# Attention of a hybrid decoder step: two heads of a pair side by side in the matmul array, V stationary, probabilities scaled before their transposes

## The reference, cut to what matters

```python
ATTN_PATTERNS = ((128, 1), (512, 4), (2048, 16))      # window, dilation; 8 heads of 64 each
def dilated_mixer(u, past, w_qkv, w_o):
    qkv = (u @ w_qkv).reshape(b, l, 3, 3, 8, 64)       # group, q/k/v, head, 64
    for g, (win, dil) in enumerate(ATTN_PATTERNS):
        s = q @ k.T + alibi bias, keys by stride dil within win
        lse = logsumexp(s); p = exp(s - lse); o_g = p @ v
    w = softmax over the groups of their lse
    return sum_g(w_g * o_g) @ w_o
```

## Time and profile before

| | us |
|---|---|
| median of 3 runs | 2786.29 (2784.93 to 2808.14) |
| profiled execution, own time | 2783.1 |
| its span | 2781.0 |
| TensorE busy in the span | 2640.1 (95%) |
| VectorE, ScalarE, GpSimd busy | 1672.3, 1275.4, 877.5 |
| the four attention turns, with the last projection | 1938.1 to 2360.5 |

### The profile page before, as it was taken

The page is one execution under the profiler, slowest core; times in us unless marked ns, Lnnn a source line. Parts: engine busy times, 40 slices in busy tenths (PEclk is TensorE's granted clock), DMA queues, the critical chain, the costliest instruction groups (busy, mean ns, idle before and its releaser), DMA issues.

```text
span 2781.0 us, 48966 instructions
## 1 busy us (share of the span) xinstructions
PE 2640.1 (95%) x19399; PEld 2551.3 (92%) x19399; DVE 1672.3 (60%) x2599; ACT 1275.4 (46%) x2139; POOL 877.5 (32%) x677
## 2 busy tenths in 40 slices
PE   6999998999999977999998999999999998899997
PEld 6999998899999967999998999998989886899997
DVE  6744757777777767843756835753343445772674
ACT  6634732444444436743736734632222224662561
POOL 4232233444444423232234232233222220423222
PEclk9999999999999988999999999999999999999999
DMA  6644622222222214644625635625222221562652
GB/s 165 160 118 126 154 82 95 79 87 70 80 91 84 92 65 130 166 114 122 169 90 132 161 110 129 157 77 181 99 96 103 87 90 42 136 160 95 152 137 73
DMA packets 92108, 316.77 MB, mean 114 GB/s; under 512 B 12240, under 2 KB 13904, under 8 KB 77456
## 3 DMA queue, kind: packets, MB, share of 16 engines
q1 hardware_dynamic: 52752, 242.78, 25.3%
q0 software_dynamic: 39168, 71.32, 15.2%
HBM read 223.44 MB, written 19.32 MB: 87 GB/s over the span
## 4 chain that ended last, share of the span: by engine, by line
PE 81%; DVE 7%; issue 4%; ACT 3%; POOL 2%; DMA 1%; SPq 0%; DVEq 0%; POOLq 0%; ACTq 0%
PE ps L1289 11%; PE ps L1281 11%; PE ps L1283 11%; PE ps L1306 7%; PE ps L1307 7%; PE ps L1313 7%; PE ps L1209 5%; PE ps L1215 5%; PE ps L1210 5%; PE ps L1618 1%; PE ps L1561 1%; PE ps L1475 1%; POOL sb_wl L600 1%; PE ps L1476 1%; PE ps L1477 1%
## 5 line engine op out<-in xcount | busy, mean ns | idle before, releaser
L1283 PE MATMUL ps<-sb_ual,sb_hw 128*128 128x288 f32 x2240 | 619.8, 297 | 0.0
L1281 PE MATMUL ps<-sb_uah,sb_hw 128*128 128x288 f32 x2240 | 618.1, 299 | 1.2 <-ACT sb_hw L789 0.8
L600 POOL TENSOR_TENSOR sb_wl<-sb_raw,sb_wh 128x1024 fp32r<-128x1024 f32 (+1 forms) x106 | 267.6, 2529 | 571.5 <-ACT sb_wh L758 571.5
L644 POOL DMA_DIRECT2D sb_lw<-sb_rawf x240 | 207.1, 864 | 703.8 <-ACT sb_lw L790 683.8
L1281 PEld LDWEIGHTS ps<-sb_uah,sb_hw 128*128 128x128 f32 x2240 | 425.4, 190 | 2.4 <-ACT sb_hw L789 2.0
L1283 PEld LDWEIGHTS ps<-sb_ual,sb_hw 128*128 128x128 f32 x2240 | 424.2, 189 | 0.0
L1289 PE MATMUL ps<-sb_uah,sb_lw 128*128 128x288 f32 x2240 | 391.0, 297 | 12.8 <-DMA sb_lw<-sb_rawf 12.8
L1209 PE MATMUL ps<-sb_uh,sb_wh 128*128 128x256 f32 (+1 forms) x1360 | 377.3, 305 | 8.9 <-ACT sb_wh L758 6.4
L1306 PE MATMUL ps<-sb_hh,sb_hw 128*128 128x288 f32 x1408 | 381.0, 298 | 4.4 <-DVE sb_x L1926 4.4
L1307 PE MATMUL ps<-sb_hl,sb_hw 128*128 128x288 f32 x1408 | 381.1, 297 | 0.0
L1210 PE MATMUL ps<-sb_ul,sb_wh 128*128 128x256 f32 (+1 forms) x1360 | 372.7, 300 | 0.0
(11 more groups left out here) (269 smaller groups left out, 5024.1 us busy)
## 6 DMA issues: line engine op xcount, KB each, us to landing
sb_rawf<-w_ffn_in SPq DMA_DIRECT2D x88, 1024.0 KB, 4.9
sb_lw<-sb_rawf POOLq DMA_DIRECT2D x272, 256.0 KB, 3.6
sb_raw<-w_ssd SPq DMA_DIRECT2D x64, 512.0 KB, 3.5
sb_rawf<-w_ffn_out SPq DMA_DIRECT2D x32, 768.0 KB, 4.2
sb_rawf<-w_ffn_out SPq DMA_DIRECT2D x32, 640.0 KB, 3.8
sb_raw<-w_att SPq DMA_DIRECT2D x40, 512.0 KB, 3.9
sb_h<-state SPq DMA_DIRECT2D x8, 1024.0 KB, 4.9
ssm_sample<-sb_h SPq DMA_DIRECT2D x8, 1024.0 KB, 4.8
```

Source lines behind the costliest of these rows:

```text
L600: pool.tensor_tensor(wl[parity][:, 0:width], raw[:, parity, 0:width], wh[parity][:, 0:width].bitcast(F32), ALU.subtract).then_inc(wl_done, 1)
L644: pool.dma_start(slot(lw, p), rawf[:, s % 2, i * BL:(i + 1) * BL], accum_op=ALU.add).then_inc(ld_in[i], 16)
L1281: pe.matmul(out, w[:, k * P:(k + 1) * P], uah[:, SIDE[p], k, :], start=begins and k == 0, stop=False, skip_group_check=True)
L1283: pe.matmul(out, w[:, k * P:(k + 1) * P], ual[:, SIDE[p], k, :], start=False, stop=False, skip_group_check=True)
```

## The change

- `scores` becomes `wide_scores(t)` and `narrow_scores(t)`: for a block t of queries both heads follow each other, head 0 in rows 0 to 63 of the array, head 1 in rows 64 to 127, each into a bank of its own.
- `normalize(e)` scales the probabilities `pr` (768 wide) by the reciprocal sum before they are transposed; `head_out`, `un` and the four transposes of `un` are gone.
- The twelve transposes of a block t go in three groups of four (`transposes(t, i)`), and ScalarE copies each group with one 512-wide copy (`probs_out(t, i)`). But for the last block and the last turn all groups use bank 2.
- `values(t)`: V is stationary (64 columns for each head, head 1 in columns 64 to 127), 128 columns of transposed probabilities move. The output has features on partitions, so `heads_out(t)` and `heads_low(t)` make its high and low part for the projection, strided into token order.
- Both sample stages go through the sequences in the order `BY_STRIP`, so that neighbours are in different strips. The sample group's own scores go into bank 2 with a step `sample_own` of their own.
- The output projection takes halves of 288 columns in token order, and VectorE adds each block to `x` with one operation.
- Order: in the first three turns `ahead(2t)` comes first in block t, then transposes and the next scores between them, then `ahead(2t+1)` and `values(t)`.

```diff
+BY_STRIP = (0, 2, 4, 6, 1, 3, 5, 7)
...
-                        nc.scalar.copy(pt[:, e % 2, 0:512], ps[:, 6, :])
-                        nc.scalar.copy(pt[:, e % 2, 512:768], ps[:, 7, 0:256]).then_inc(pt_done, 1)
+                        src = ps[:, turned_bank(t, i, last), :]
+                        if i == 1:
+                            nc.scalar.copy(pt[:, :, 512:768], two(src)).then_inc(pt_done, 1)
+                        else:
+                            nc.scalar.copy(pt[:, i // 2, 0:512], src).then_inc(pt_done, 1)
+
+                    def heads_out(t):
+                        act.wait_ge(pv_mm, c * 4 + (t + 1))
+                        nc.scalar.copy(perm(oh[:, 0:SEQ])[:, t, :], ps[:, head_bank(last), 0:P]).then_inc(oh_done, 1)
...
+                    def wide_scores(t):
+                        if t:
+                            pe.wait_ge(max_done, c * 8 + 2 * t)
+                        for j in range(2):
+                            r = slice(HD * j, HD * j + HD)
+                            pe.matmul(ps[:, 4 + j, :], qkv[r, 0, rows(t)], qkv[r, 1, 0:SEQ], start=True, stop=True)
...
+                        pe.wait_ge(pt_done, c * 12 + (3 * t + 3))
...
                         for k in range(6):
-                            v = vt[:, max(0, k - 3), k if k < 4 else t, r]
-                            ins = pe.matmul(ps[:, 2, 0:HD], pt[:, e % 2, rows(k)], v, start=k == 0, stop=k == 5)
+                            for j in range(2):
+                                r = slice(HD * j, HD * j + HD)
+                                v = vt[:, max(0, k - 3), k if k < 4 else t, r]
+                                ins = pe.matmul(ps[r, head_bank(last), 0:P], v, pt[:, j, rows(k)], start=k == 0, stop=k == 5)
...
-                            for b in range(NB):
-                                out = ps[32 * (b // 2):32 * (b // 2) + 32, 3, 0:P]
-                                for k in range(4):
+                            for k in range(4):
+                                for b in BY_STRIP:
+                                    out = ps[32 * (b // 2):32 * (b // 2) + 32, 3, 0:P]
...
+                        for t in range(CH):
+                            if t:
+                                pe.wait_ge(q_evac, c * 9 + (9 + 2 * t))
+                            ahead(2 * t)
+                            sample_step(2 * t)
+                            transposes(t, 0)
+                            if t < CH - 1:
+                                wide_scores(t + 1)
+                            transposes(t, 1)
+                            if t < CH - 1:
+                                narrow_scores(t + 1)
+                            transposes(t, 2)
+                            pe.wait_ge(q_evac, c * 9 + (10 + 2 * t))
+                            ahead(2 * t + 1)
+                            sample_step(2 * t + 1)
+                            values(t)
...
+                        V.tensor_scalar(pr[:, e % 2, :], pr[:, e % 2, :], rcp[:, e:e + 1], None, ALU.mult).then_inc(norm_done, 1)
...
+                        V.tensor_tensor(perm(ol[:, 0:SEQ])[:, t, :], ps[:, head_bank(last), 0:P],
+                                        perm(oh[:, 0:SEQ])[:, t, :].bitcast(F32), ALU.subtract).then_inc(ol_done, 1)
...
-                        xm = x[:, m, 0:SEQ].rearrange("p (a h t) -> p h t a", h=2, t=2)
-                        V.tensor_tensor(xm, xm, ps[:, b:b + 2, 0:QTR].rearrange("p h (t a) -> p h t a", t=2), ALU.add)
-                        V.tensor_tensor(x[:, m, SEQ:TOK], x[:, m, SEQ:TOK], ps[:, b + 1, QTR:QTR + SMP],
-                                        ALU.add).then_inc(ao_evac, 1)
+                        V.tensor_tensor(two(x[:, m, :]), two(x[:, m, :]), ps[:, b:b + 2, 0:HALF], ALU.add).then_inc(ao_evac, 1)
```

More of the change, by code:

```diff
@@ L250, in step_kernel @@
             stage = at("stage", [P, AHEAD, TOK])
-            un = at("un", [P, CH, P])
             oh = at("oh", [P, TOK], F32R)
@@ L1158, in sample_step @@
                             ins.then_inc(soh_done, 1)
[L1160 to L1175, removed]
+                    if last:
+                        for t in range(CH):
+                            for i in range(3):
+                                probs_out(t, i)
+                            sample_step((1, 2, 4, 6)[t])
+                            heads_out(t)
+                            if t < CH - 1:
+                                exps(2 * t + 2)
+                                exps(2 * t + 3)
+                                sample_step((6, 3, 5)[t])
+                    else:
+                        for t in range(CH):
+                            ahead(2 * t + 1)
+                            sample_step(2 * t)
+                            for i in range(3):
+                                probs_out(t, i)
+                            ahead(2 * t + 2)
+                            if t < CH - 1:
+                                exps(2 * t + 2)
+                                exps(2 * t + 3)
+                            sample_step(2 * t + 1)
+                            heads_out(t)
                         ahead(9)
@@ L1554, in ahead, with narrow_scores @@
                         product(c * 10 + u, u % 2, KD, uh, ul, (0, 1), SPLIT)
[L1556 to L1568, removed]
+                    def wide_scores(t):
[4 more added lines that the diff above has]
+                            pe.matmul(ps[:, 4 + j, :], qkv[r, 0, rows(t)], qkv[r, 1, 0:SEQ], start=True, stop=True)
+                    def narrow_scores(t):
+                        for g in (1, 2):
+                            for j in range(2):
+                                r = slice(HD * j, HD * j + HD)
+                                ins = pe.matmul(ps[:, 6 + j, rows(g - 1)], qkv[r, 3 * g, rows(t)],
+                                                qkv[r, 3 * g + 1, rows(t)], start=True, stop=True)
+                        ins.then_inc(sc_mm, 1)
                     pe.wait_ge(q_evac, c * 9 + 9)
@@ L1608, in values @@
[L1608 to L1616, removed]
-                            v = vt[:, max(0, k - 3), k if k < 4 else t, r]
-                            ins = pe.matmul(ps[:, 2, 0:HD], pt[:, e % 2, rows(k)], v, start=k == 0, stop=k == 5)
+                    wide_scores(0)
@@ new lines, in turn, with transposes @@
+                    narrow_scores(0)
+                    for g in range(AG):
+                        ins = pe.transpose(ps[0:SMP, 2, rows(g)], qkv[:, 3 * g + 2, SEQ:TOK], ident[:, :])
+                    ins.then_inc(vt_mm, 1)
+                    sample_scores()
+                    def transposes(t, i):
+                        n, bank = 3 * t + i, turned_bank(t, i, last)
+                        if i < 2:
+                            pe.wait_ge(norm_done, c * 8 + (2 * t + i + 1))
+                        if n == 0:
+                            pe.wait_ge(own_done, c + 1)
+                        elif t == CH - 1 and i:
+                            pe.wait_ge(max_done, c * 8 + 8)
+                        elif last:
+                            pe.wait_ge(pt_done, c * 12 + max(1, n - 1))
+                        elif i:
+                            pe.wait_ge(pt_done, c * 12 + n)
+                        else:
+                            pe.wait_ge(ol_done, c * 4 + t)
+                        for q, (j, k) in enumerate((((0, 0), (0, 1), (0, 2), (0, 3)), ((0, 4), (0, 5), (1, 4), (1, 5)),
+                                                    ((1, 0), (1, 1), (1, 2), (1, 3)))[i]):
+                            ins = pe.transpose(ps[:, bank, rows(q)], pr[:, j, rows(k)], ident[:, :])
+                        ins.then_inc(pt_mm, 1)
@@ new lines, in values @@
+                    def values(t):
+                        pe.wait_ge(pt_done, c * 12 + (3 * t + 3))
+                        if last and t:
+                            pe.wait_ge(ol_done, c * 4 + t)
+                        for k in range(6):
+                            for j in range(2):
+                                r = slice(HD * j, HD * j + HD)
+                                v = vt[:, max(0, k - 3), k if k < 4 else t, r]
+                                ins = pe.matmul(ps[r, head_bank(last), 0:P], v, pt[:, j, rows(k)], start=k == 0, stop=k == 5)
@@ L1648, in turn @@
                     if last:
[L1650 to L1656, removed]
-                    else:
[L1658 to L1674, removed]
+                        wide_scores(1)
+                        narrow_scores(1)
+                        for t in range(CH):
+                            for i in range(3):
+                                transposes(t, i)
+                            sample_step((0, 2, 4, 0)[t])
+                            values(t)
+                            if t < CH - 2:
+                                wide_scores(t + 2)
+                                narrow_scores(t + 2)
+                            sample_step((0, 3, 5, 0)[t])
+                    else:
```

(44 more changed lines are left out.)

145 lines of the change are left out of this document (70 added, 75 removed).

## The result

The changed kernel takes 2706.95 us (median of 4 runs, 2702.87 to 2707.93) against 2789.82 before (4 runs); the ratio is 0.9689, 95% interval 0.9642 to 0.9735. The profiled execution took 2702.87, its span is 2700.8. The forecast was 2713, 2698 to 2750.

What follows compares the result with a forecast made beforehand. TensorE was taken to bound the loop's three turns, the chain between engines the last. Three times -18.5 and -18 made -73.5: 2783.1 to 2709.6, plus 3.2 for the median of runs, 2713; range 2698 to 2750.

Steps and rivals of the forecast that it cites:

- the sum: All terms together: three turns of the loop -55.5, last turn with its projection -18, all -73.5 us.
- Values: Values of a block: the two heads' records run two at a time, 1.4 us, -5.4 a turn (bounds 0 and -5.4).
- Scores: Scores of a block: the heads' row groups overlap, 1.8 us in place of 3.0, -4.8 a turn (bounds 0 and -5.6).
- The rival without overlap: In the loop, score pairs don't run side by side: 2728; this or value pairs failing 22%, both 10%.
- Strip order: Both sample stages, neighbours in different strips: 2.3 us each from 5.28 and 5.92, -6.6 a turn (bounds -4.2 and -7.7).
- The projection: Output projection ending a loop turn: plain addition makes it TensorE-bound, 6.5 us in place of 9.2, -2.7 a turn.
- Added waits: New waits on TensorE's queue: +0.3 three times for bank 2, +0.9 at a turn's head; +1.8 a turn (+0.5 to +4).
- Scaling in the loop: VectorE's scaling of the probabilities in the loop's blocks: hidden, so costs nothing; uncovered it would be 1.8 a block.
- The last turn: Last turn up to its projection, bounded by VectorE's chain: 38.1 us in place of 53.5, -15.4 (bounds -10 and -17).
- the 5.0 at the end: Last turn, behind the last scaling: two groups of transposes, copies, values and the high and low parts, 5.0 us.
- The last projection: Projection after the last turn, VectorE-bound, 15.9 us: 0.58 less on each of eight blocks, partly overlapped, -2.6.
- The rival that ends slower: TensorE falls to half clock, 1.2 GHz, in the loop's turns after new waits; two turns give about 2813; 3%.

Runs made afterwards that it cites:

- control: The changed kernel itself, run again with nothing changed as a measure for the others: 2710.58 us, ratio 0.9734 against the kernel before.

## Why the prediction was right

The bound was read rightly: TensorE's own operations in the loop's turns, the chain between engines in the last. In the loop I had -18.5 a turn; measured -18.2, -19.6 and -20.9. Only turn 0 has a granted clock of 1.00 in both traces. The third turn of the kernel before, which the rows above leave out:

```profile
2171.10:2287.30 116.20, 114.54 (x822) 0.96 0.27 93
```

So the second and third turn went from 0.97 and 0.96 to 0.99 and 0.98, and the 1.4 and 2.7 us that they gave beyond turn 0 go with that. What the change itself gave in the loop is then about 54.6 of the 58.7 us (an estimate: three times turn 0), against 55.5 foretold.

The spans shrank by 80.2 us where the sum said 73.5. The 6.7 more are 3.2 in the loop, 1.1 in the last projection, 2.5 by which the attention stage began sooner and 0.9 behind it, less 0.9 in the last turn. None of them is a gain of the mechanism that the sum had missed; the first two go with the clock.

- Values: 1.4 a block foretold, 1.46 measured. What I took from the earlier trace rows, seven records in flight where one strip meets the next, held for halves of 64 columns, and the order by heads confirmed it.
- Scores: 1.8 a block foretold from 1.6 to 3.0. Wide 1.06, narrow 0.65 with its change of shape, and the transposes between them 0.15 longer each time: 1.9. The rival without overlap fell in the experiment with the wide scores apart.
- Strip order: 2.3 a stage foretold, 1.87 and 1.88 measured, near the bound of 1.75. The term was mis-sized by 0.9 a turn: it is -7.5, not -6.6.
- The projection: 6.5 foretold, 7.5 measured. I took the slower of the two engines and left out that with two pairs of banks they wait for each other. With three pairs it is 6.6. The term was -1.7 a turn, not -2.7. This miss and that of the strips nearly cancel, and that the loop's sum is so close is in part luck.
- Added waits, the term of +1.8: the wait at a turn's head was put at 0.9 and is 0.74. The one for bank 2 was put at 0.3; between the end of the copy, 1951.32 + 0.59, and the next transposes at 1951.96 it shows, but it costs 0.2 at most with the change of shape that is due anyway. Together that is about 1.3 (an estimate: 0.74 and three times 0.2).
- Scaling in the loop: covered, as foretold, with more room than I worked out.
- The last turn: 15.4 foretold, 14.5 (control: 16.1) measured, but not by the parts named. I put eight scalings, 7.2 us, on the chain. Without the scaling the turn is 0.5 shorter, and only two of the eight are on the control's chain (0.62 and 0.63). This step of the prediction was wrong. In place of the scalings stand TensorE's operations for which VectorE waits: 13.3 us of that chain's 41.1 are TensorE's (its rows added up), scores and transposes of 2.6 behind a block's maxima at full clock among them, and I had put TensorE only into the 5.0 at the end. The last turn's sum was right by luck: two errors met.
- The last projection: -2.6 foretold, -3.7 measured. From its first matmul to its last addition it is 15.7 in the kernel before, 14.6 with the permuted additions put back and 12.0 in the changed kernel: the additions are worth the 2.6. The other 1.1 goes with the clock. Its start in the kernel before, in the changed kernel (whole), and in the one with the wide scores apart:

```profile
2344.61:2347.80 3.19, 3.19 (x13) 0.51 0.03 5
```

```profile
2268.97:2280.99 12.02, 10.47 (x69) 1.00 0.08 13
```

```profile
2280.64:2285.90 5.26, 5.26 (x22) 0.50 0.01 3
```

  The last of these has the changed kernel's projection and took 13.3 for it, as did the one with three pairs, which also began with 5 us at half clock; the seven others with this projection began at full clock and took 12.0.
- The clock: in the loop's turns it was 1.00, 0.99 and 0.98 where it had been 1.00, 0.97 and 0.96. The rival that ends slower did not come about; the clock rather added to the gain, which no term of the sum had.

## What to carry to other kernels

Small matmuls that use half or a quarter of the array cost what they do because their neighbours use the same part. Look for the seam between two parts in the trace, count the records in flight there, and if they double, alternate the parts in program order, matmul by matmul; the seam is all that a block order gets. Where two engines pass a few blocks to and fro, the slower engine's time is the bound only with enough buffers. And of a chain with a wait, write down every operation that must stand in it: one that lies beside another adds nothing.

## What the runs showed of the hardware

Halves and quarters of the array took fp32 matmuls side by side with nearly no loss: two row groups 1.06 for 1.05, two column halves 1.46 for 24 records of 0.11, four strips 1.88 for 64. The page "TensorE: Matmul & The Clock Gate" of the Trainium skill (Part 3, The mechanism) has loads overlap only with matmuls of another row group. The values and the sample stages use the same rows throughout, and yet 24 records take 1.46 us and not 24 x 0.11, so the trace disagrees.

A copy on VectorE took six times as long beside an operation on GpSimd. In the kernel before, three copies of 576 columns from SBUF to SBUF took 3.40 us beside a subtraction on GpSimd; in the changed one they take 450 ns each; in turn 0 GpSimd is idle beside them. First the line's shortest, median and longest copy (ns) and the timeline of turn 0 before, then the line after:

```profile
L2325 DVE COPY sb_qkv<-sb_stage x9: 449/453/2671, 2036.0 to 2274.2; 128x576 f32<-128x576 f32 x9
...
2035.99 3.40 DVE L2325 COPY sb_qkv<-sb_stage 128x576 f32<-128x576 f32 x3
...
2036.38 2.70 POOL L600 TENSOR_TENSOR sb_wl<-sb_raw,sb_wh 128x1024 fp32r<-128x1024 f32 x1 [6.18 <-ACT sb_wh L758]
```

```profile
L2385 DVE COPY sb_qkv<-sb_stage x9: 448/450/452, 2007.4 to 2205.0; 128x576 f32<-128x576 f32 x9
```

One of three copies lasts 2671 ns, as long as GpSimd's operation. It was hidden under `ahead(8)` and cost nothing here: VectorE then waited for TensorE until 2041.16. That GpSimd is the cause was not tried by a run of its own.
